# Gathers of a mixture of experts: empty rooms get an index beyond the last row instead of row 0

## The reference, cut to what matters

```
order = argsort(expert)                      # 2048 (token, expert) pairs
buf   = zeros(...).at[dest].set(h[tok_sorted])   # rows of one expert side by side, padded
y     = (silu(xb @ w_gate[e]) * (xb @ w_up[e])) @ w_down[e]     # per block of rows
out   = zeros(n, d).at[tok_sorted].add(y[dest] * w_sorted)
```

```
layer 0: 239 201 199 152 129 121 92 70 70 67 65 61 61 54 45 40 39 36 35 35 34 34 34 28 21 19 18 16 14 8 6 5
layer 1: 221 170 147 111 85 83 81 80 74 69 64 62 60 59 55 54 48 47 46 44 42 40 37 37 35 34 32 32 31 29 28 11
```

## Time and profile before

| | |
|---|---|
| median of three runs | 3045.5 us |
| the profiled execution's own time | 3050.79 us |
| its span | 3049.3 us |
| mean granted TensorE clock | 0.947 |
| TensorE busy | 2681.9 us, 88% of the span |
| DMA | 605.21 MB, mean 198 GB/s |
| experts of layer 0, from the first gather to the last product | 921.57 to 1527 us |
| experts of layer 1 | 2415.75 to 3000 us |

### The profile page before, as it was taken

The page is one execution under the profiler, slowest core; times in us unless marked ns, Lnnn a source line. Parts: engine busy times, 40 slices in busy tenths (PEclk is TensorE's granted clock), DMA queues, the critical chain, the costliest instruction groups (busy, mean ns, idle before and its releaser), DMA issues.

```text
span 3049.3 us, 35536 instructions
## 1 busy us (share of the span) xinstructions
PE 2681.9 (88%) x13504; PEld 1342.7 (44%) x13504; DVE 1164.9 (38%) x2901; ACT 663.2 (22%) x1646; POOL 361.6 (12%) x433
## 2 busy tenths in 40 slices
PE   3999999999958999999849998999999489899972
PEld 2455944444533334333324774555544334334421
DVE  5223927455352222222261113777743522122214
ACT  3214710000111111111041002655622111111111
POOL 1000000000001111110031211222500111111102
PEclk9999999999978999999979999999999599999996
DMA  8221015535029999999842110000000699999997
GB/s 287 110 75 57 2 37 168 195 124 195 28 105 342 387 349 337 382 380 350 354 165 95 43 55 28 29 29 34 25 21 28 228 379 374 367 363 351 374 396 290
DMA packets 203953, 605.21 MB, mean 198 GB/s; under 512 B 57089, under 2 KB 111881, under 8 KB 154505
## 3 DMA queue, kind: packets, MB, share of 16 engines
q1 hardware_dynamic: 147192, 531.32, 46.4%
q0 software_dynamic: 56592, 71.62, 7.3%
HBM read 554.58 MB, written 47.98 MB: 198 GB/s over the span
## 4 chain that ended last, share of the span: by engine, by line
PE 72%; DMA 14%; DVE 10%; issue 2%; ACT 2%; SPq 1%; POOL 0%; DVEq 0%; POOLq 0%; ACTq 0%
PE ps L1784 16%; DMA R<-in_w_up 10%; PE ps L979 7%; PE ps L1746 7%; PE ps L2430 6%; PE ps L473 4%; PE ps L1215 3%; PE ps L983 3%; PE ps L2427 3%; PE ps L2927 2%; PE ps L479 2%; PE ps L2705 2%; PE ps L2709 1%; PE ps L785 1%; DVE XR L2043 1%
## 5 line engine op out<-in xcount | busy, mean ns | idle before, releaser
L1784 PE MATMUL ps<-R 128*64 128x512 f32 (+1 forms) x3872 | 652.4, 533 | 69.1 <-DMA R<-in_w_up 63.2
L1784 PEld LDWEIGHTS ps<-R 128*64 128x64 f32 (+1 forms) x3872 | 216.0, 129 | 424.1 <-issue 383.9
L1746 PE MATMUL ps<-R 128*64 128x512 f32 (+1 forms) x1936 | 309.8, 509 | 1.8 <-DVE R L1608 1.8
L979 PE MATMUL ps<-R 128*128 128x512 f32 x512 | 225.9, 600 | 5.6 <-DMA R<-in_w_in 5.0
L1671 ACT ACTIVATE R<-ps,small 128x64 f32<-128x64 f32 (+1 forms) x256 | 87.0, 420 | 598.9 <-PE ps L1717 598.9
L1746 PEld LDWEIGHTS ps<-R 128*64 128x64 f32 (+1 forms) x1936 | 107.0, 126 | 189.3 <-issue 172.3
L1636 DVE TENSOR_TENSOR R<-ps,R 64x512 f32<-64x512 f32 (+1 forms) x97 | 59.9, 617 | 336.6 <-PE ps L1784 216.3
L1608 DVE COPY R<-ps 128x256 f32<-128x256 f32 (+1 forms) x97 | 37.9, 391 | 341.9 <-PE ps L1728 341.9
L979 PEld LDWEIGHTS ps<-R 128*128 128x128 f32 x512 | 97.7, 192 | 129.6 <-issue 123.0
L1685 ACT ACTIVATE R<-ps 64x512 f32<-64x512 f32 (+1 forms) x97 | 52.4, 541 | 468.6 <-PE ps L1784 468.6
L1811 POOL DMA_INDIRECT R<-XN,xidx x52 | 52.2, 1004 | 757.8 <-DVE R L1412 739.9
(11 more groups left out here) (361 smaller groups left out, 3839.8 us busy)
## 6 DMA issues: line engine op xcount, KB each, us to landing
R<-in_w_gate SPq DMA_DIRECT2D x128, 1024.0 KB, 19.7
R<-in_w_up SPq DMA_DIRECT2D x128, 1024.0 KB, 21.9
R<-in_w_down SPq DMA_DIRECT2D x128, 1024.0 KB, 23.8
R<-in_w_ada SPq DMA_DIRECT2D x40, 1024.0 KB, 5.5
R<-in_w_in SPq DMA_DIRECT2D x7, 2048.0 KB, 16.9
R<-in_w_in SPq DMA_DIRECT2D x13, 1024.0 KB, 5.4
YE<-R POOLq DMA_DIRECT2D x42, 256.0 KB, 19.4
R<-in_w_ada SPq DMA_DIRECT2D x4, 2048.0 KB, 15.6
```

What stands on the lines that cost most here:

```text
L979: i_ = T.matmul(o, wv[:, kk, cols], k.hT[:, kk, tk], start=kk == 0, stop=kk == 7)
L1746: i_ = T.matmul(k.ps[r * j:r * j + r, 5 + b % 2, 0:n], v.hT[b % 2][:, c:c + r], w[:, kk % 2, n * j:n * j + n], start=kk == 0, stop=kk == 3)
L1784: i_ = T.matmul(hidden_out(k.ps[P0 + r * j:P0 + r * j + r, b % 2, 0:n], r), x_, hidden_columns(w, r, j), start=kk == 0, stop=kk == 7)
```

## The change

Empty rooms get the index 2048 instead of 0. The constant `tok` is the token less 2048, so that the table holds token - 2048 in a filled room and 0 in an empty one, and the two casts become additions of 2048. All three gathers get a bound of 1023 and leave out rows beyond it. The number and the order of the instructions on every engine are unchanged.

```
+NO_ROW = 2048
...
-    add("tok", 128 * np.arange(8)[None, :] + p)
+    add("tok", 128 * np.arange(8)[None, :] + p - NO_ROW)
...
-    V.tensor_copy(k.xidx[0:64, 0:NBLK], k.ps[0:64, 1, 0:NBLK]).then_inc(*rt.up())
-    V.tensor_copy(k.xidx[64:128, 0:NBLK - 1], k.ps[64:128, 1, 1:NBLK]).then_inc(*rt.up())
+    V.tensor_scalar(k.xidx[0:64, 0:NBLK], k.ps[0:64, 1, 0:NBLK], float(NO_ROW), None, ALU.add).then_inc(*rt.up())
+    V.tensor_scalar(k.xidx[64:128, 0:NBLK - 1], k.ps[64:128, 1, 1:NBLK], float(NO_ROW), None, ALU.add).then_inc(*rt.up())
...
         G.indirect_dma_start(v.xb[t % XBUF][0:n], None, k.XN[L],
-                             bass.IndirectOffsetOnAxis(ap=k.xidx[0:n, at // 2:at // 2 + 1], axis=0)
+                             bass.IndirectOffsetOnAxis(ap=k.xidx[0:n, at // 2:at // 2 + 1], axis=0),
+                             bounds_check=1023, oob_is_err=False
                              ).then_inc(*s[f"d_xt{t % XBUF}"].up(16))
...
```

More of the change, by code:

```diff
@@ L1836, in gpsimd_experts @@
     n0 = P.places
-    G.indirect_dma_start(v.xl[0:64], None, k.XN[L], bass.IndirectOffsetOnAxis(ap=k.xidx[0:64, n0:n0 + 1], axis=0)
+    G.indirect_dma_start(v.xl[0:64], None, k.XN[L], bass.IndirectOffsetOnAxis(ap=k.xidx[0:64, n0:n0 + 1], axis=0),
+                         bounds_check=1023, oob_is_err=False
                          ).then_inc(k.loop[L]["x"], 16)
@@ L1925, in gpsimd_loop @@
         G.indirect_dma_start(v.xl[0:64], None, k.XN[L],
-                             bass.IndirectOffsetOnAxis(ap=k.xidx[0:64, NBLK:NBLK + 1], axis=0)).then_inc(o["x"], 16)
+                             bass.IndirectOffsetOnAxis(ap=k.xidx[0:64, NBLK:NBLK + 1], axis=0),
+                             bounds_check=1023, oob_is_err=False).then_inc(o["x"], 16)
         G.wait_ge(o["ve"], j * 4 + 8)
```

## The result

The kernel after takes 3006.53 us in the median of four runs (3001.81 to 3009.86); the kernel before, run beside it, 3046.57 us in four. The profiled execution of after took 3005.17 us, with a span of 3003.5 us and a mean granted clock of 0.951.

The account below looks back on a forecast made before the run. Full DMA stretches, where TensorE waits for weights, were taken as the bound: 25.3 us of relief, three quarters arriving (19 us), plus 1 us of clock and edits at 0, gave -20 us, 3025.5 us against the median; range 3014 to 3044 us.

Parts of the forecast that it names:

- What bounds the kernel: Expert stages: DMA engines set the end only in full stretches, where TensorE waits for weights; elsewhere TensorE sets the pace.
- What is left out: Gathers of both layers and the loop: 1600 rows, 6.55 MB of the 71.62 MB on GpSimd's queue.
- rival (2): Gathers: nothing is left out, a row beyond the bound or something its size still moves; 3045.5 us, chance 0.09.
- The price of a row: Full stretches: a row left out gives 0.022 us in 64-row gathers, 0.0097 us in 128-row ones; together 25.3 us.
- the cap: Layer 0, 921 to 953 us: rows worth 4.5 us counted as 2.2, since TensorE waits only 2.17 us there.
- near 400: Expected sign: GB/s while 64-row gathers with half their rows pass; nearly full ones still at 320.
- The share that arrives: Full stretches: three quarters of 25.3 us, 19 us, since a DMA running ahead meets 14 full places earlier.
- The prediction's upper bound of 25.3 us: Relief of the full stretches if all of it arrives; lower bound 12.7 us if every second microsecond is lost.
- The clock: Matmuls after waits: a wait short enough to keep 2.4 GHz gives 2.6 us; bounds 0 and 5, taken 1 us.
- Edits at nothing: Casts made additions, another tok constant, the gathers' bound check: taken as 0 us.
- rival (3): GpSimd: the bound check makes gathers dear, delaying first gathers and stores; 3062 us at 6 us each, chance 0.09.
- Rival (1), uneven relief: 64-row gathers: empty rooms mostly in rows 32 to 63 relieve half the engines; 3 to 4 us, 3042 us, chance 0.18.

Follow-up runs that it names:

- e8: Kernel before, every row still moved, but rows 32 to 63 of each 64-row tile go to partitions 64 to 95: 3005.75 us, ratio 0.9866.
- e3: Kernel after, but rows left out only of the 128-row gathers and the loop's second gather; other empty rooms fetch row 0: 3049.27 us, ratio 1.0008.
- e11: Kernel before with idle matmuls (4 or 7) ahead of five long waits for weights, each filling shorter than its wait: 3041.65 us in 12 runs, ratio 0.9989.
- e4: Kernel after, but 64-row tiles' gathers also leave out partitions 32 to 63, full or not: 3035.55 us, layer 1 routed otherwise.
- e5: Kernel after, but 64-row tiles' gathers also leave out partitions 0 to 31, full or not: 3102.46 us, layer 1 routed otherwise.
- e6: Kernel after, but no gather fetches any row and products use what lies in the buffers: 3126.01 us, layer 1 routed otherwise.

## Why the prediction was right or wrong

**What bounds the kernel: right.** The gain is in the waits for weights of the full stretches, 36.0 us in place of 63.2 where some 45 were named, and the loop's w_down wait went with them.

**What is left out: right.** 6.54 MB of the 6.55, all 1600 rows; rival (2) falls by the page's bytes.

**The price of a row: right in kind, too small in size.** This is the first failing step. The relief can be read from the windows as the prediction priced it: the bytes left out at 423 GB/s, and the length of the stretch times the gain in speed. For 1210 to 1363 us, 270 rows are 2.6 us and 150 x (1 - 380/398) = 6.8 us, together 9.4 where I had 5.5. In the same way 990 to 1109 gives 4.5 (3.3), 1150 to 1175 1.1 (0.8) and 922 to 953 3.6 (4.5); in layer 1 3.3 (3.1), 5.4 (3.5) and 2.8 (2.2), and for the last stretch, with the rates divided by their DMA shares of 1.01 and 0.98, about 8.7 (4.7). That is 39 us against the 27.6 that the rows came to before the cap, though the stretches of the two kernels are matched only roughly. The 0.78 us a gather came from the first five 64-row gathers of layer 1 alone. The same price can be read from e8 over the long stretches: 150 x (1 - 380/408) = 10.3 us for the seven 64-row gathers from 1210 us on, 119 x (1 - 390/401) = 3.3 us for four from 990 us on, and in layer 1 115 x (1 - 372/405) = 9.4 us for seven and 60 x (1 - 381/411) = 4.4 us for four. That makes 1.25 us a gather in the mean, from 0.8 to 1.5, where the prediction had 0.78 (an estimate, with the same rough matching). The whole says so too: 43 gathers of 64 rows at 0.78 us are 33.5 us if every one counts, and e8, which moves all their bytes, wins 41 us net of longer transposes (292 for 275 ns each, 280 of them in the trace, 5 us if all of it showed). That a gather's cost falls row by row was assumed and is not borne out at the start: with 21 of 128 rows left out the first two gathers of layer 1 run at 317 GB/s, no faster than before (321), and with one half of their partitions alone at 353 and 365, not "near 400". Why a later gather costs more than the first ones is open. The part for 128-row gathers was wrong the other way: 0.0097 us counted for each, nothing measured (e3).

**The share that arrives: the second failing step.** I took three quarters of 25.3 us, 19. The waits fell by 36.2 us, nine tenths of the relief of 39. The 39 us rest on the rough matching of the stretches, so how the error divides between price and share is less certain than the 36.2 us themselves. That places which fill earlier lose little, since little of the full stretches is DMA idle time, is my reading and was not tested; so is that the cap of 2.2 us at 921 to 953 was wrong, because what TensorE does not wait for there fills places ahead and later waits shrink. The prediction's upper bound of 25.3 us held the price fixed and bounded the conversion only; a price measured in one place needs bounds of its own. SyncE's waits for TensorE were not longer, as I had said, but 144.3 for 152.0 us and 270.9 for 270.7 in layer 0.

**The clock: undersized.** 1 us was forecast; the same matmuls are 9.6 us shorter in layer 0 and 2.3 longer in layer 1, 7.3 together. How much of that is a gain of its own is not settled: filling the waits with products (e11) gives 9 us in layer 0 of one execution, but 3 us by the ratio of all its runs, with no gain inside the interval.

**Edits at nothing: right.** 0.23 us for the additions, 0.05 us more for a gather, the first gather's wait 9.9 and 10.7 us; rival (3) needed 2.5 us a gather.

**Rival (1), uneven relief: refuted.** It allowed 3 to 4 us, and the waits fell by 36.2; in e4 and e5 either half of the rows slows the others. The descriptor map had been read too freely for it. In the Trainium skill, "DMA: Bandwidth & Descriptors", section "The descriptor swizzle", an engine writes four rows of 0 to 31 and the four that lie 32 higher in a transfer to 128 partitions, so by that map rows 32 to 63 relieve the same engines as rows 0 to 31, and not another half of them. e4 and e5 (353 and 365 GB/s) do not contradict this; which engine carries which row of a 64-row gather no row here shows. The remark beside it, that the shared ports are what crowds, agrees with e8, which does not show a port; the prediction had it as another way to the same 25 us, not as a reason for a larger price.

**Size.** The gain was twice the forecast. The sizes are one chain: the relief 39 us, not 25.3; nine tenths of it, not three quarters; 7 us of matmul time, not 1: 43.5 us in the profiled executions, 40 in the medians.

## What to carry to other kernels

Padding rows of a 64-row gather are worth leaving out when a stream of weights runs beside it and TensorE waits for that stream. Ask first where, and how wide, the gather writes: in this kernel a 64-row gather on partitions 0 to 63 cost the stream much more than its bytes (321 for 423 GB/s), and the same rows on 0 to 31 and 64 to 95, by a gather of 128 indices, cost it little (414), with every byte still moved. To price such a disturbance, measure the stream's rate over the long full stretches and not over the first few transfers alone, and bound the price as well as the share of it that arrives. Padding rows of the 128-row gathers were worth nothing here.

## What was not expected of the hardware

- While the first two 64-row gathers of layer 1 pass on partitions 0 to 63, all that the DMA engines move falls from 423 to between 317 and 321 GB/s; on partitions 0 to 31 and 64 to 95 it is 414 GB/s, with the same bytes (e8), and 412 with no row at all (e6).
- A row left out of a gather stays as a packet under 512 B (58688 for 57089 of them); the number of packets on GpSimd's queue is 56592 as before.
- Rows left out of 128-row gathers gave back nothing (e3), though the DMA engines were full in the stretches that hold most of them.
- A wait of 3.39 us was followed by 16 matmuls at full speed, one of 3.25 us in the other kernel by 16 at a granted clock of 0.54. What decides is open.
